# Joined attention with the query tiles taken from the last to the first

## What is computed

```python
def nsa_block(q, g, q_pos, kc, vc, kc_end, ks, vs, kw, vw, kw_pos):
    s_c = einsum(q, kc); p_c = masked_softmax(s_c, kc_end <= q_pos); o_c = einsum(p_c, vc)   # 63 compressed keys
    s_s = einsum(q, k_sel); p_s = masked_softmax(s_s, pos_sel <= q_pos); o_s = einsum(p_s, v_sel)
    s_w = einsum(q, kw); p_w = masked_softmax(s_w, 0 <= q_pos - kw_pos < WINDOW); o_w = einsum(p_w, vw)
    return g0 * o_c + g1 * o_s + g2 * o_w

b_out = lax.map(query_block, (arange(n_qb), q_b, g_b))      # 8 blocks of 128 queries, each for itself
```

## Time and profile before

| | us |
|---|---|
| median of 3 runs | 1378.63 (1378.39 to 1382.24) |
| the profiled execution | 1379.65 |
| its span | 1377.7 |
| joined attention, first scores to last product | 478.3 to 898.4 |
| PE busy over the span | 1160.5 |
| DVE busy over the span | 820.7 |

### The profile page before, as it was taken

The page is one execution under the profiler, slowest core; times in us unless marked ns, Lnnn a source line. Parts: engine busy times, 40 slices in busy tenths (PEclk is TensorE's granted clock), DMA queues, the critical chain, the costliest instruction groups (busy, mean ns, idle before and its releaser), DMA issues.

```text
span 1377.7 us, 17323 instructions
## 1 busy us (share of the span) xinstructions
PE 1160.5 (84%) x6863; PEld 934.6 (68%) x6863; DVE 820.7 (60%) x1398; ACT 381.0 (28%) x794; POOL 413.6 (30%) x343
## 2 busy tenths in 40 slices
PE   4777777499999739888988998979969999978996
PEld 3777777499988524445454554558849999977884
DVE  3699999999995457854544455453443670055333
ACT  2211010011211545463444545440111121144000
POOL 2322222000004084543243332354331222215444
PEclk9888888799999958998999999989989999988998
DMA  7534441211213170003012040262222111031221
GB/s 244 195 117 129 137 130 53 53 31 46 46 31 151 33 261 2 1 1 153 1 60 95 1 153 1 92 152 92 81 65 61 46 46 46 15 128 61 77 99 46
DMA packets 78577, 111.29 MB, mean 81 GB/s; under 512 B 21198, under 2 KB 65870, under 8 KB 75237
## 3 DMA queue, kind: packets, MB, share of 16 engines
q1 hardware_dynamic: 72725, 75.90, 17.6%
q0 software_dynamic: 3712, 33.56, 6.6%
q10 hardware_dynamic: 2080, 1.05, 0.3%
HBM read 96.71 MB, written 18.74 MB: 84 GB/s over the span
## 4 chain that ended last, share of the span: by engine, by line
PE 54%; DVE 33%; ACT 4%; issue 3%; DMA 3%; POOL 2%; SPq 0%; POOLq 0%; DVEq 0%; ACTq 0%
PE PS L1456 14%; PE PS L1593 14%; DVE Y L537 9%; PE PS L1004 6%; DVE CTMP L477 5%; PE PS L885 5%; PE PS L1018 3%; DVE CTMP L480 3%; PE PS L606 3%; PE PS L980 2%; DVE AB L484 2%; DVE CTMP L481 2%; DVE CTMP L483 2%; PE PS L939 1%; DVE PS L1099 1%
## 5 line engine op out<-in xcount | busy, mean ns | idle before, releaser
L606 PE MATMUL PS<-XH,WH 128*128 128x352 f32 (+1 forms) x648 | 148.6, 340 | 82.1 <-POOL WL L269 51.1
L606 PEld LDWEIGHTS PS<-XH,WH 128*128 128x128 f32 (+1 forms) x648 | 113.6, 195 | 88.7 <-POOL WL L269 52.6
L537 DVE SCALAR_TENSOR_TENSOR Y<-U,SM,Y 128x1024 f32<-128x1024 f32 x120 | 144.7, 1281 | 0.0
L606 PE MATMUL PS<-XL,WH 128*128 128x352 f32 (+1 forms) x648 | 144.3, 332 | 0.0
L606 PE MATMUL PS<-XH,WL 128*128 128x352 f32 (+1 forms) x648 | 143.8, 332 | 0.0
L606 PEld LDWEIGHTS PS<-XL,WH 128*128 128x128 f32 (+1 forms) x648 | 113.7, 194 | 1.4
L606 PEld LDWEIGHTS PS<-XH,WL 128*128 128x128 f32 (+1 forms) x648 | 113.0, 193 | 1.4
L269 POOL TENSOR_TENSOR WL<-WRAW,WH 128x1024 fp32r<-128x1024 f32 (+1 forms) x15 | 46.3, 3095 | 215.6 <-DVE WL L269 181.8
L1004 PE MATMUL PS<-KV,Q 64*128 64x512 f32 (+3 forms) x384 | 85.3, 524 | 30.0 <-ACT PRS L1045 28.8
L885 PE MATMUL PS<-PT,TM 128*64 128x256 f32 x528 | 90.8, 424 | 18.8 <-DVE PT L1032 13.7
L1456 PE MATMUL PS<-WOH,XH 128*128 128x512 f32 (+1 forms) x288 | 94.7, 411 | 13.5 <-POOL WOL L1427 7.0
(11 more groups left out here) (289 smaller groups left out, 2155.4 us busy)
## 6 DMA issues: line engine op xcount, KB each, us to landing
WRAW<-in_w_in_even SPq DMA_DIRECT2D x16, 512.0 KB, 4.7
WRAW<-in_w_in_odd SPq DMA_DIRECT2D x16, 512.0 KB, 3.9
XIN<-in_x_prompt SPq DMA_DIRECT2D x8, 512.0 KB, 5.7
WB<-in_w_cmp SPq DMA_DIRECT2D x1, 4096.0 KB, 13.7
WRAW<-in_w_in_even SPq DMA_DIRECT2D x16, 256.0 KB, 3.7
TM<-in_state_win_kv SPq DMA_DIRECT2D x8, 512.0 KB
XR<-in_x_prompt SPq DMA_DIRECT2D x8, 512.0 KB, 3.4
layer_out<-R SPq DMA_DIRECT2D x8, 512.0 KB, 2.6
```

The lines of the kernel that those rows point to most:

```text
L537: ins = v.scalar_tensor_tensor(dst, src, CWT[:, i, t:t + 1], dst, ALU.mult, ALU.add)
L606: ins = pe.matmul(PS[0:mcols, b0 + c, 0:CH], w[:, slot, kk, 0:mcols], x[:, kk, c * CH:(c + 1) * CH], start=(kk == 0 and n == 0), stop=(kk ...
```

## The change

The query tiles are taken from qt = 7 down to qt = 0. Two places that worked out a unit's place from qt now count the units themselves. Nothing else is edited; the planner runs over the new list, so the order of every engine's attention steps is another, as are the places of the sample steps between them.

```diff
-        UNITS = [(qt, gp, br) for qt in range(SEQ // P) for gp in range(2) for br in (SELBR, WINB, CMPB)]
+        UNITS = [(qt, gp, br) for qt in reversed(range(SEQ // P)) for gp in range(2) for br in (SELBR, WINB, CMPB)]
@@ def values(t, u, i):
-                n = 2 * qt + gp
+                n = u // 3
                 if first and n:
                     pe.wait_ge(s_om, n)
@@ for ev in ORDER: (DVE)
                 elif ev[0] == "O":
-                    qt, gp = ev[1] // 2, ev[1] % 2
+                    qt, gp, _ = UNITS[3 * ev[1]]
                     o = BG[:, 2 * gp:2 * gp + 2, tok(qt)]
```

## The result

The reversed order takes 1384.09 us (1380.64 to 1386.39, 16 runs), the kernel before beside it 1378.72 (1373.90 to 1385.05, 16 runs); the ratio is 1.0033 [1.0022, 1.0043]. That is 4.5 us more (3.0 to 5.9 by the interval; the two medians differ by 5.4), just past the 4.1 us that the prediction takes as the least that can be told from no change. The forecast was 1379.6, "even", with 1374.5 to 1382.8 for that case, and the range 1370 to 1389. The profiled execution took 1381.81 us with a span of 1379.9, before 1379.65 and 1377.7.

The account below looks back on a forecast made before the run. Of the joined attention's 393 us, 330 is PE's work at full clock and 63 is loss. Terms 3.0 + 0 - 6.0 + 1.5 + 2.5 sum to +1.0 us: 1379.6 against the runs, range 1370 to 1389.

Parts of the forecast that it names:

- even: Whole time 1374.5 to 1382.8 us: head's idle time and tail pay for the vanished run at 640; chance 0.39.
- The head: Attention's start, 505.5 to first turn near 522.5: tile 7's pairs wait for each other, loss 14.3 against 10.0, net +3.0 us.
- the credit of 1.3 us for the first pair: At the head: the first pair's 1.99 us of PE work goes under the wait at 478, gaining 1.3 us.
- The clock at the head: Half clock through the head, back 5 us into the dense turns behind it; half clock until 525 to 530.
- The slower rival: 1388 us, +9.5 in all: head's half clock lasts 11 us or more into the turns; chance 0.34.
- the rule that I had set beside rows 7: PE's clock swings when briefly idle while PSUM banks cycle; taken to keep the head at half clock, giving 1388.
- The rank steps: Samples' rank steps on DVE, now among turns of qt = 7: same DVE time, 0 us; ends -4 and +4.
- my high end: For the rank steps: +4 us if every step holds up a turn.
- The run at 640: 640 to 660, six pairs of qt = 4 nearly without turns: vanishes, -6.0 us; ends -8 and 0.
- Small pairs and tail: Runs of 512, 256 and 128 keys, +1.5 us; last six units with one turn each, +2.5 us.
- The faster one: 1370 us, -9 in all: clock back by the first turn, the run's whole 8 us gained; chance 0.27.

Follow-up runs that it names:

- e11: Reversed order with the second pair scored into spare PSUM banks 4 to 7, before the masks: 1378.57 us, ratio 1.0001 to the kernel before.
- e9: Reversed order with the samples' rank comparisons replaced by a fill with zeros: 1377.53 us, ratio 0.9996 to the kernel before.
- e10: Kernel before, tiles still rising, with the samples' rank comparisons replaced by a fill with zeros: 1368.37 us, ratio 0.9919.
- e5: Reversed order with each rank step held back on DVE until the next even turn's copy: 1379.10 us, ratio 1.0006 to the kernel before.
- e1: Kernel before with query tiles in the order 0, 1, 2, 7, 6, 5, 4, 3: 1368.91 us, ratio 0.9937.
- e3: Kernel before with tile 7 put first, then rising from 0 to 6: 1397.07 us, ratio 1.0153.
- e7: Tile order 1, 0, 2, 7, 6, 5, 4, 3 with rank steps held back behind the next even turn's copy: 1371.15 us, ratio 0.9955 to the kernel before.

## Why the prediction was right, and where its sum was off

The range held the time and the signs of all large terms were right. The sum was +1.0 us and the measurement +4.5, which put the result outside the even case. The head was too small, a wait in the next 40 us was missing, and the credit of 1.3 us for the first pair isn't seen. That the sum came as near as it did is in part luck: it also lacked the 2.5 us gained from 160 to 200 us.

*The head, a loss of +4.3 forecast (+3.0 with the credit of 1.3), +5.1 measured.* The mechanism was right: one pair waits for the other, from 505.40 to 511.80, 516.96 and 521.74, 6.4, 5.2 and 4.8 us each where 4 to 4.8 had been forecast, with 1.5 us of idle time in each. PE is idle for 5.4 us between 505.4 and the first turn (6.5 forecast). The first turn came at 524.1, not 522.5, and as this execution's masks were done 1.7 us earlier, it came 22.6 us behind DVE's first maximum instead of 19.3. Part of the excess was outside my window, which began at 505.5. Behind the masks DVE and ACT first have 1024 keys instead of 128. In the changed kernel:

```profile
501.48 1.23 DVE L1099 CUSTOM_DVE_ANT_0 PS<-PS,MASKC 128x1024 f32<-128x1024 f32 x1 [5.23 <-POOLq L1233]
```

From here to PE's next scores at 505.40 it is 3.9 us; before, from 503.24 to 505.48, 2.2. I worked that chain out (503.24 to 506.2, 3.0 us), but charged only the pairs behind it. These 1.7 us are more than what the term was short of. e11 gives 4.4 us back, 2.0 of which can be the scores that it moves.

*The clock at the head, back 5 us into the turns by forecast.* PE alone in the changed kernel:

```profile
526.00:528.00 2.00, 2.00 (x9) 0.50 0.00 0
528.00:530.00 2.00, 2.00 (x13) 0.75 0.00 0
```

The clock went from 1.2 to 2.4 GHz near 529, 5 us after the first turn at 524.1. The slower rival needed 11. So at the head the excess is idle time, 5.7 us of it, and not the clock, of which the head loses slightly less than before, 9.1 against 9.7; in the next 40 us the clock does lose 1.6 us more. Nor did the time come out by the rule that I had set beside rows 7 (Trainium skill, "TensorE: Matmul & The Clock Gate", "A second HAM failure mode: psum-queue depth-cycling"). That section of the Trainium skill says that the clock swings between its levels where PE idles for short times between groups while PSUM banks are cycled. That it would stay at the lower one through the head and 11 us into the turns was my reading and isn't stated there: here the clock was at 0.50 through three gaps of 1.5 us and rose soon behind them, and 1388 wasn't reached.

*The rank steps, 0 forecast, +2.7 measured in that stretch.* I added up DVE's time, some 17 of 23 us, and found room. A share says nothing of order: an in-order engine that is three quarters busy still delays one copy by whatever stands ahead of it. As the price of the rank steps the 0 holds: by e9 and e10 they cost 8.6 us of this stretch in the reversed order and 8.1 before. What the sum put at nothing are tile 7's own maxima ahead of a copy, the stops of 1.68 and 1.39 us, which stay when the comparisons go. Steps that hold up turns, the case of my high end, are there in both orders, with 3.6 and 3.7 us of waits, and e5 gets 3.7 us back in this one.

*The run at 640, -6.0 forecast, -6.5 measured* (4.4 us against 10.9 from 120 to 160 us). Right, in place and size. Its removal is also in e1, where it isn't paid for at the head.

*Small pairs and tail, +1.5 and +2.5 forecast, +3.5 measured from 280 us on.* Right together. (Before, nine turns follow the last scores at 886.57, not 14; the loss of 1.0 us there was read from the row and stays.) From 880 to 900 PE is busy for 17.41 us, 87%, as forecast. The last turn follows its scaling by 0.1 us, and the output weights weren't late. The changed kernel's last steps on POOL, PE and ACT:

```profile
897.82 1.58 POOL L1248 TENSOR_SCALAR PRC<-PRC,STAT,GTOK 128x63 f32<-128x63 f32 x4
...
899.46 0.65 PE L1018 MATMUL PS<-ident,PRC 128*63 128x128 f32 x4 [0.16 <-POOL PRC L1248]
...
900.64 3.88 ACT L1415 ACTIVATE WOH<-WOR 128x1024 fp32r<-128x1024 f32 x4
...
904.26 1.01 PE L1456 MATMUL PS<-WOH,XH 128*128 128x512 f32 x2 [2.82 <-POOL WOL L1427]
```

From the end of the attention (901.9) to the output projection it is 2.4 us, as before.

*The rivals.* The faster one needed a cheap head, and had -8 for the run; the run gave 6.5 and the head cost 5.1. What stays open: how much of the rank's price in the order before is its place, how e11's 4.4 us divide, where e10's larger gain lies, the 1.7 us of PE work, and why e3 loses 7 us or more beyond head and run. Its table shows both idle time and clock from 80 us on, without one large stop that I could name.

## What to carry to other kernels

Before permuting a planned order, price its three places apart: what the first item holds up while the other engines are cold, what the last item leaves uncovered, and which side work each item now stands beside. Falling sizes cover the next item's start-up with the last one's turns, but start with small items: (0, 1, 2, 7, 6, 5, 4, 3) gives 0.9937, where the plain reversal gives 1.0033. One small tile in front wasn't enough here: 1.0106 with tile 0, 1.0033 with tile 2. On an in-order engine put side work right behind the copy that the bottleneck waits for, not ahead of it, and then look what it waits for next (3.7 us gained in the reversed order, nothing in e7), and lend the first items buffers that only later work needs (4.4 us).

## What the runs showed of the hardware that I had not expected

PE's clock isn't a fixed cost of a stretch. Before, PE stayed at 1.2 GHz through 20 us of dense work with tiles 0 and 1; after, with a quarter of the head idle, it rose 5 us behind the first turn. In 25 runs of the kernel before on one chip, time and the mean granted clock go together with a correlation of -0.79, some 0.76 us for each 0.001 of the clock, and e10's six runs spread from 1362.6 to 1374.0. Differences of 2 to 3 us between two profiled executions are thus no proof of anything. What an edit gains rests on ratios of several rounds; the table's differences by stretch come from one execution each, and what is said of their causes rests on the waits named beside them.
